# Dilated attention over tokens ordered by parity, with 128 instead of 256 keys per query tile in two of three groups

## The reference

```python
DIL_PATTERNS = ((128, 1), (512, 4), (2048, 16))
...
    for gi, (win, dil) in enumerate(DIL_PATTERNS):
        o, lse = strided_window_attn(q[:, :, gi], k[:, :, gi], v[:, :, gi], win // dil, dil)
...
    w = jax.nn.softmax(jnp.stack(lses, axis=0), axis=0)
    o = jnp.sum(w[..., None] * jnp.stack(outs, axis=0), axis=0)
```

## Time and profile before

| | |
|---|---|
| median of 3 runs | 2386.62 us (2386.52 to 2386.75) |
| the profiled execution, from first to last instruction (its span; no other time is given for it) | 2392.7 us |
| TensorE matmul busy | 2183.2 us, 91% of the span |
| VectorE, ScalarE, GpSimd busy | 657.4, 356.8, 121.6 us |
| projections of the dilated branch | about 1812 to 1949 us |
| dilated attention, with what comes right behind | 1955.6 to 1988.9 us |

### The profile page before, as it was taken

How to read it: one execution, slowest core, us unless ns; L and a number is a source line. 1 busy time by engine, 2 the same in 40 slices (tenths; PEclk the granted TensorE clock), 3 DMA queues, 4 the chain that set the end, 5 groups by cost and what they waited for, 6 DMA issues and landing times. The chain is left out here.

```text
span 2392.7 us, 27727 instructions
## 1 busy us (share of the span) xinstructions
PE 2183.2 (91%) x11542; PEld 1346.1 (56%) x11542; DVE 657.4 (27%) x1482; ACT 356.8 (15%) x830; POOL 121.6 (5%) x164
## 2 busy tenths in 40 slices
PE   6987898999999986999889998897599999989998
PEld 2554664656566543444455554454376458858863
DVE  2143332422222213313531111111455330034201
ACT  2043431200000001112420000000131122011000
POOL 4000000010000001000000000000110000000000
PEclk9998999999999998999989999999899999999999
DMA  9364173799999997521199999999643433443441
GB/s 333 121 222 154 37 280 124 279 420 420 420 420 419 421 420 296 208 70 53 54 362 420 419 420 419 420 419 411 213 153 124 136 106 106 150 141 126 147 154 40
DMA packets 154309, 601.75 MB, mean 252 GB/s; under 512 B 15289, under 2 KB 19073, under 8 KB 103488
## 3 DMA queue, kind: packets, MB, share of 16 engines
q1 hardware_dynamic: 144512, 582.98, 63.1%
q0 software_dynamic: 8144, 11.57, 1.5%
q10 hardware_dynamic: 1520, 5.32, 0.6%
HBM read 589.84 MB, written 21.23 MB: 255 GB/s over the span
## 5 line engine op out<-in xcount | busy, mean ns | idle before, releaser
L366 PE MATMUL psum<-ring,h_t 128*128 128x512 f32 (+1 forms) x1024 | 429.3, 581 | 4.9 <-ACT h_t L1072 2.1
L366 PEld LDWEIGHTS psum<-ring,h_t 128*128 128x128 f32 x1024 | 192.4, 192 | 234.8 <-issue 229.9
L399 PE MATMUL psum<-h_t,ring 128*128 128x256 f32 (+1 forms) x1424 | 311.4, 381 | 4.6 <-ACT ff_hid L2572 2.3
L399 PEld LDWEIGHTS psum<-h_t,ring 128*128 128x128 f32 (+1 forms) x1424 | 270.2, 190 | 45.4 <-issue 3.6
L2386 PE MATMUL psum<-ring,h_t 128*64 128x256 f32 x2272 | 260.4, 382 | 3.1 <-DMA ring<-in_expert_w_dram 2.1
L2386 PEld LDWEIGHTS psum<-ring,h_t 128*64 128x64 f32 x2272 | 158.1, 137 | 88.6 <-issue 11.7
L2386 PE MATMUL psum<-wide,h_t 128*64 128x256 f32 x1664 | 192.7, 385 | 2.3 <-DMA wide<-in_expert_w_dram 1.5
L2386 PEld LDWEIGHTS psum<-wide,h_t 128*64 128x64 f32 x1664 | 115.7, 138 | 67.5 <-issue 9.0
L337 DVE COPY h_t<-psum 128x512 f32<-128x512 f32 (+2 forms) x76 | 50.4, 663 | 317.2 <-PE psum L1940 290.7
L1940 PE MATMUL psum<-gates,h_row_tiles 128*128 128x256 f32 (+1 forms) x512 | 104.8, 359 | 1.4 <-ACT h_row_tiles L337 1.4
L1940 PEld LDWEIGHTS psum<-gates,h_row_tiles 128*128 128x128 f32 x512 | 85.6, 190 | 20.6 <-issue 10.4
(11 more groups left out here) (590 smaller groups left out, 2090.4 us busy)
## 6 DMA issues: line engine op xcount, KB each, us to landing
ring<-in_expert_w_dram SPq DMA_DIRECT2D x210, 1024.0 KB, 24.5
wide<-in_expert_w_dram SPq DMA_DIRECT2D x156, 1024.0 KB, 25.6
ring<-in_ada_w_dram SPq DMA_DIRECT2D x48, 1024.0 KB, 10.8
ring<-in_w_in_dram SPq DMA_DIRECT2D x30, 1024.0 KB, 5.3
ring<-in_diff_w_in_dram SPq DMA_DIRECT2D x12, 1024.0 KB, 16.0
gates<-in_expert_w_dram SPq DMA_DIRECT2D x12, 1024.0 KB, 27.5
x<-in_expert_w_dram SPq DMA_DIRECT2D x12, 1024.0 KB, 28.1
ring<-in_w_gate_dram SPq DMA_DIRECT2D x12, 1024.0 KB, 5.1
```

Source lines behind the costliest of these rows:

```text
L366: mm = k.nc.tensor.matmul(banks[r][0:m, 0:nn], lhs(k0 + j, r), w[:, j, :], start=(k0 + j == 0), stop=(k0 + j == k_tiles - 1))
L399: mm = k.nc.tensor.matmul(banks[i][0:h, 0:n_rhs], w[:, j, b:b + h], rhs(k0 + j), start=(k0 + j == 0), stop=(k0 + j == k_tiles - 1))
```

## The change

The tokens of the dilated branch are taken in another order: first the 128 even places, then the 128 odd ones. Tile 0 is now the even tokens, tile 1 the odd.

- `of_parity` gives the projections every second column of `h_t` as stationary operand; the positions are loaded so that partition p of tile i has token 2p + i.
- In the groups with dilation 4 and 16, a tile of queries meets the 128 keys of its own tile. In the group with dilation 1 it still meets all 256. A unit's row has 256 + 128 + 128 = 512 scores instead of 768; the mask is laid out to match.
- The final copies put the tokens back in order (`in_order`), writing at a step of two elements.
- `attention` lets the score matmuls of a unit differ in width. For the other four attentions that makes the same instructions.

```diff
--- before.py
+++ after.py
@@ -648,11 +648,14 @@
                 if i >= 2:
 
                     pe.wait_ge(*exps_done(i - 2))
-                w = units[i]["qk"][0][1].shape[-1]
+                c = 0
                 for a, (q, kk) in enumerate(units[i]["qk"]):
-                    c = w * units[i].get("place", range(heads * 3))[a]
+                    w = kk.shape[-1]
+                    if "place" in units[i]:
+                        c = w * units[i]["place"][a]
                     mm = nc.tensor.matmul(s_view(i)[:, c:c + w], q, kk, start=(c % BANK == 0), stop=True,
                                           skip_group_check=True)
+                    c += w
                 mm.then_inc(scores_ready.sem, 1)
 
             def turn(i):
@@ -858,8 +861,10 @@
     q, kk = tok[:, None], tok[None, :]
     swa = np.where(np.abs(q - kk) <= 128, 0.0, NEG)
     swa = np.concatenate([swa, np.zeros((S, S))], 1).astype(f)
-    dil = np.concatenate([np.where((q >= kk) & ((q - kk) % d == 0) & (q - kk <= 128 * d), 0.0, NEG)
-                          for d in (1, 4, 16)], 1).astype(f)
+    split = np.concatenate([tok[0::2], tok[1::2]])
+    reach = lambda d: np.where((q >= kk) & ((q - kk) % d == 0) & (q - kk <= 128 * d), 0.0, NEG)[split][:, split]
+    same = lambda a: np.concatenate([a[0:P, 0:P], a[P:S, P:S]], 0)
+    dil = np.concatenate([reach(1), same(reach(4)), same(reach(16))], 1).astype(f)
     i16 = np.arange(P) % 16
     lag = (i16[:, None, None] - np.arange(16)[None, :, None] == np.arange(16)[None, None, :]).astype(f)
     fold = (np.arange(P)[:, None] % 32 == np.arange(32)[None, :]).astype(f)
@@ -965,8 +970,7 @@
                  "head_is": t["head_is"], "parity_is": t["parity_is"], "within_chunk": t["within_chunk"]}
     late["fold_pick"] = fold_pick
     late_loads = [(late[name][:], src) for name, src in late_from.items()]
-    late_loads += [(late["positions"][:, i:i + 1], t["positions_2"][0, i * P:(i + 1) * P].unsqueeze(1))
-                   for i in range(T_LAT)]
+    late_loads += [(late["positions"][:], t["positions_2"][0].rearrange("(p i) -> p i", i=T_LAT))]
     x_dram = t["x"][0].rearrange("(t p) d -> p t d", p=P)
     ctx_dram = t["ctx"][0].rearrange("(t p) d -> p t d", p=P)
     vec = lambda a: a.rearrange("(r c) -> r c", c=P)
@@ -2735,7 +2739,8 @@
     by_two = lambda a: a.rearrange("p (b s) -> p b s", b=2)
     z, u, k_in = by_two(x[:, 2, 0:BANK]), by_two(x[:, 2, BANK:D]), by_two(x[:, 3, 0:BANK])
     k_row = x[:, 3, BANK:D].rearrange("p (i b d) -> p i b d", i=T_LAT, b=2)
-    mask = x[:, 2:4, :].rearrange("p t d -> p (t d)")[:, 0:6 * S].rearrange("p (t k) -> p t k", t=T_LAT)
+    mask = x[:, 2:4, :].rearrange("p t d -> p (t d)")[:, 0:4 * S].rearrange("p (t k) -> p t k", t=T_LAT)
+    of_parity = lambda kt, i: h_t[:, kt, 0:S].rearrange("p (s i) -> p i s", i=T_LAT)[:, i, :]
     qk_lag = lambda lag: h_t[:, 2 * (lag % 4):2 * (lag % 4) + 2, S:2 * S]
     o_t, sq = h_t[:, 0:4, S:2 * S], h_t[:, 4:8, S:2 * S]
     y_at = lambda i, h: h_t[:, 2 * i + h // 2, S + P * (h % 2):S + P * (h % 2) + P]
@@ -2978,7 +2983,7 @@
                 if n0 < 3072:
                     return rope_out(k, bank, zd[:, r, n0:n0 + nn], t1, tabs[:, r, 0, :], tabs[:, r, 1, :], P)
                 return copy_by(k, who, vv[:, r, n0 - 3072:n0 - 3072 + nn], bank)
-            dil_groups = project_groups(k, lambda kt, r: h_t[:, kt, r * P:(r + 1) * P], DK, [P] * T_LAT, 4608,
+            dil_groups = project_groups(k, of_parity, DK, [P] * T_LAT, 4608,
                                         out_of_psum, lambda r, n0: "dve" if n0 < 3072 else "act")
 
             def turn_s(i):
@@ -3060,13 +3065,17 @@
         for i in range(T_LAT):
             for h in range(4):
                 units.append(dict(
-                    qk=[(q_t[:, 4 * g + h, i * P:(i + 1) * P], k_t[:, 4 * g + h, :]) for g in range(3)],
-                    v=[vv[:, j, (4 * g + h) * P:(4 * g + h + 1) * P] for g in range(3) for j in range(T_LAT)],
+                    qk=[(q_t[:, 4 * g + h, i * P:(i + 1) * P], k_t[:, 4 * g + h, slice(0, S) if g == 0 else slice(
+                        i * P, (i + 1) * P)]) for g in range(3)],
+                    v=[vv[:, j, (4 * g + h) * P:(4 * g + h + 1) * P] for g in range(3) for j in
+                       (range(T_LAT) if g == 0 else (i,))],
                     mask=mask[:, i, :], sink=None, out=y_at(i, h).rearrange("p (x y d) -> p x y d", x=1, y=1)))
         k.need(mask_loaded)
-        attention(k, "dil", units, P ** -0.5, 1, 3 * S, P)
+        attention(k, "dil", units, P ** -0.5, 1, 2 * S, P)
+        in_order = lambda b: br_t[:, 2, b, :].rearrange("p (s i) -> p i s", i=T_LAT)
         banks_phase(k, transpose_groups(k, [([y_at(i, b) for i in range(T_LAT)],
-                                             lambda who, bank, b=b: copy_by(k, who, br_t[:, 2, b, :], bank))
+                                             lambda who, bank, b=b: copy_by(k, who, in_order(b), bank.rearrange(
+                                                 "p (i s) -> p i s", i=T_LAT)))
                                             for b in range(4)]))
```

## The result

| | before | changed |
|---|---|---|
| median | 2386.75 us (19 runs, 2383.05 to 2394.32) | 2379.13 us (19 runs, 2374.85 to 2387.03) |
| ratio, 95% interval | | 0.9965 (0.9957 to 0.9974) |
| the profiled execution's span | 2392.7 us | 2376.9 us |
| its own time | | 2378.2 us |
| first scores of the dilated attention to the first product behind it | 33.32 us (1955.63 to 1988.95) | 24.68 us (1948.30 to 1972.98) |

By the ratio the change is worth 0.35%, that is 8.4 us, with an interval of 6.2 to 10.3; the two medians are 7.6 us apart, the means 8.3. Forecast were 2377.8 us, a range of 2375.0 to 2381.0, and a gain of 8.8 us. The two spans differ by 15.8 us, nearly twice that. In the trace they part like this: 8.64 us within the attention, 7.3 us before it, where both kernels issue nearly the same instructions. The second part is no gain of the change, as the experiments show.

A forecast was written before the change was run, and what follows sets the result against it. The attention was taken as bound by TensorE except at its start. Savings of 0.9 (start), 2.5 (scores) and 5.3 us (transposes, values) made 8.8 with rounding, so 2386.62 became 2377.8 us, range 2375.0 to 2381.0.

The forecast's parts named there:

- The start: Start of the dilated attention, 5.34 us: unit 0's scores save 0.42, the maximum 0.27, the exponential 0.23; sum 0.9 us saved.
- Scores, transposes and values: TensorE's work per attention unit: scores save 0.42 us, 2.5 in six body units; transposes and values 0.67, 5.3 in eight.
- the other bound: Scores of 128 columns: no gain, 216 ns each instead of the 112 taken, giving back 2.9 us.
- The attention as a whole: Dilated attention: 8.8 us saved in sum, about 22.2 us in place of 31.0.
- Cover for ScalarE and VectorE: Their work in the body fits beside 2.21 us units with 1.4 us to spare; the tail's last copy only just covered.
- The rival by which latency takes TensorE's place: VectorE and ScalarE's chain sets unit time, body stays at 3.29 us, only 2.7 us gained: 2383.9 us; chance 0.04.
- Strides, cost 0: Projections' weights read and final copies written at a step of two elements: no cost taken for either.
- The two bounds: For strided weight loads and final copies: no change, or ScalarE's ratio 1.86, giving loads of 354 ns or copies 0.6 us.
- The rival in which the loads become the bound: Projections: strided weight loads outlast 427 ns of streaming, gain gone at 458 ns; 2419 us at 570 ns; chance 0.03.
- The clock: One 3.4 us half-clock stretch after TensorE's start gap, 1.7 us lost, kept in both kernels; rival that it falls otherwise 0.20.
- The two upward bounds: Additions allowed for in the range: 2.9 us for the narrow scores, 0.6 us for the final copies.
- The comparison of the span with the median: Whole kernel before: runs' median 6.1 us below the profiled span of 2392.7 us; saving subtracted from the median 2386.62.

## Why the prediction was right

**The start, right.** 5.34 us became 4.43, 0.91 against 0.92 in the sum, though its parts were off by a little: the exponential takes 721 ns and not 707.

**Scores, transposes and values, right.** 0.42, 0.22 and 0.45 us saved per unit: 1.30 to 0.88, 0.66 to 0.44, 1.34 to 0.89. The narrow score matmul costs what its columns cost; the other bound (no gain, 2.9 us back) is out. That these savings are on the path was the step that could fail, and doubling the transposes tested it: 3.50 us for eight doses of 0.44.

**The attention as a whole, right.** 33.32 to 24.68 us are 8.64 against 8.8. The attention up to its last values was summed up to 22.2 us and took 1970.69 - 1948.30 = 22.39. Each attention holds one stretch of 3.4 us.

**Cover for ScalarE and VectorE, right, and as thin at the end as said.** ScalarE idles for 0.91 us in each unit of the body. One more copy of 0.49 us went into this reserve there and came out in the tail alone, 0.66 us in all. The rival by which latency takes TensorE's place is out: with one more copy no unit of the body waits, with twenty each does.

**Strides, cost 0, right in effect.** The two bounds were no change and a ratio of 1.86; measured were 1.03 for loads (190 to 196 ns) and 1.05 for ScalarE's copies. The rival in which the loads become the bound needed 458 ns; no step tried passed 309.

**The clock: the outcome right, the reason wrong.** The prediction kept one stretch of 3.4 us in both kernels because "the runs shown, which lie within 0.23 us of each other" were to mean that it doesn't move between runs of one kernel. Those were three runs. Nineteen of the same kernel spread over 11.3 us, and with the same gap the stretch came in five profiles of nine. Here what the Trainium skill says (TensorE: Matmul & The Clock Gate, Part 1: The HAM clock gate), that the slow phase varies from run to run, fits, and the three runs misled. That both profiled executions had their stretch is luck. Had one of them had none, the two attentions would have differed by 7 or 10.3 us, still inside the range forecast. The prediction also tied the stretch to TensorE's gap alone; in the projections it comes without one, behind short products.

**The range, a little narrower than its own terms.** The two upward bounds together, 2.9 and 0.6 us, reach 2381.3 and not 2381.0, and a second stretch would add 1.7. Neither bound came true, so it didn't matter. Nor was the scatter of the runs in it: the median of 19 runs lies inside, but single runs of the changed kernel go from 2374.85 to 2387.03.

**The comparison of the span with the median, incomplete.** The span of before was 6.1 us above the median of the runs. That was one execution at the slow end of the scatter, not something that profiling adds: in every execution of the changed kernel the time is 1.2 to 1.3 us more than the span, and by that the profiled one of before took 2394.0 us, close to the slowest of its 19 runs (2394.32). The forecast did not suffer, since it subtracted a difference from the median.

**What stays open.** Whether the shorter gap keeps the clock up at this place: none of four profiles (three kernels) with a gap of 1.2 us or less had a stretch. If five stretches fell on thirteen profiles at random, these four would all be spared in 10 cases of 100, so alone that doesn't settle it. The counts over the whole traces, 20 of 213 against 129 of 247, point the same way. What decides whether a gap of 2.4 us is followed by a stretch, present in one execution and absent in the next, no run shows. What else than the clock varies in the first 1945 us was not traced to its places.

## What to carry to other kernels

Where an engine's queue runs without a wait through a stage, a change's worth there can be summed from records of the same shape, to a few per cent; look then for the one place at which a cover is thinnest, usually the end of the loop. Reordering tokens so that masks fall into whole tiles cost nothing that could be measured here, since the order could be had from a step of two elements in an access pattern. A table load at the start of a stage is on the path if that stage begins with ScalarE's answer: load it in the idle time of the stage ahead. And take the scatter of a program from more than three runs before arguing that something doesn't move.

## What the runs showed of the hardware

- A weight load of 128 columns in float32 takes 190 ns in a row and 196 at a step of 2 elements; read from another tile, 309 at 4 and 296 at 16. All of them stay hidden below 427 ns of streaming.
- The exponentials' table load of 1.28 us can be placed by a one-column activation (0.20 us), and the twelve copies in between leave the table in place.
- After a gap of 2.4 to 2.5 us in TensorE's work, a stretch of 3.4 us at half clock (1.2 GHz) followed in five profiles and not in four others, whose code up to there is the same or nearly so; it cost 1.66 us. Over all gaps of 1.9 to 2.6 us it was 129 of 247, over those of 0.9 to 1.9 us 20 of 213.
- The clock also fell to half with TensorE busy throughout: behind 13 of 26 blocks of thirty products with 32 columns.
- All in all the program spends 140 to 163 us at half clock ahead of the attention, and that amount differs from run to run.
